# A two-layer block kernel: the mixer's attention moved ahead of its recurrence, and the first loads reordered

## The chip, the cores and the metric

The kernel runs on one core of one Trainium2 chip. The metric is the time of one execution on the device in microseconds (us); lower is better. Before the change the median of three runs is 2019.54 us (2014.81 to 2019.84).

## What is computed

One sequence of 256 tokens with 1024 features, in float32, goes through a first block of two layers and a second block of two layers. A layer of the first block is:

```
x = x + 0.5 * swiglu(rms_norm(x, g1), w_in, w_out)              # ffn1
z = rms_norm(x, g2) @ mix_w_in
z_fox, z_moba, z_rwkv = split(z)
y_fox  = forgetting attention: 4 heads of 64, q and k normed, causal softmax, cumulated log gates added
y_rwkv = recurrence: 8 heads of 64; per token  state = state*w + (state @ -kk) (kk*a)^T + v k^T,  y = state @ r
         then a norm per head, a bonus term and a gate
y_moba = attention: 4 heads of 64, q and k normed, rotary turn of 16 of 64 features, causal softmax
x = x + concat(y_fox, y_rwkv, y_moba) @ mix_w_out               # mixer
x = x + attention of x over 256 memory rows: 4 heads of 128     # xa
x = x + 0.5 * swiglu(rms_norm(x, g3), w_in, w_out)              # ffn2
```

The second block (convolution, sparse attention, pooling) is not touched.

## The kernel before, in words

**Weights.** All weights come as one stream of 546 units of 256 x 512 values (0.5 MB). SyncE loads unit u into one of four slots when VectorE is done with unit u - 4. Each product is made of three float32r matmuls (high by high, high by low, low by high), so a unit is split first: ScalarE copies the rounded high half (`act_split`, L296, which waits until TensorE has used unit u - 4), VectorE subtracts for the low half (`dve_split`, L305), and TensorE then runs twelve matmuls of 512 columns (L320 to L322) or twenty-four of 256 columns with the weights stationary (L343 to L345). The splits run three units ahead of TensorE when a stage begins.

**Order.** Each engine's program is written out by hand: `pe_mix`, `act_mix`, `dve_mix` and `pool_mix` list the steps of the mixer in the order in which the engine performs them, and semaphores tie them together. An engine stands still at a step until what the step waits for has come, whatever is ready behind it. So a `dve_split(1)` or `act_split(1)` in the list is a fixed place at which a unit is split, and what is behind it waits for TensorE to have used the unit four before.

**The mixer.** It takes 28 units for the projection, 8 for keys and values of the memory (`pe_kv`), 4 and 4 for the output (wo_a for the attentions, wo_b for the recurrence). The old order of the projection is: low-rank columns (4 units, `pe_rw_low`), the recurrence's k, r and v (12 units, `pe_rw_cols`, transposed output), then the attentions' q, k and v (12 units, `pe_z`). The recurrence is computed in four chunks of 64 tokens: key lengths (`pe_rw_length` L818, `dve_rw_length` L825, a power of -1/2 on GpSimd L830, `pe_rw_spread` L839), products of keys and queries (L924), the inverse of a triangular matrix per chunk by doubling (`pe_rw_inv0`, then `pe_rw_level` 1 to 5, L984, L993 and L996, with masks and additions on VectorE L1004 and L1009), then per chunk right-hand side, solution and state (`pe_rw_rhs`, `pe_rw_early`, `pe_rw_u`, `pe_rw_state`). In the old order the attention units lie between the levels, the memory's transposes (`pe_kv_turn`) and units and the first attention (fox) between the chunks, and the second attention (moba) behind the last chunk with nothing beside it, then wo_a and wo_b.

**Attention.** Norm of q and k (square, reduction L543, power on GpSimd L559, two scalings L551 and L554), rotary turn on 16 columns per head, transposes (L578) copied by ScalarE (L584), scores (L1333, for fox with added gate sums L1337), mask and maximum on VectorE (L1350, L591), exponentials on ScalarE (L599), transposes of the probabilities (L613) copied by ScalarE or VectorE (L620, L627), values (L641) and the final scaling (L649). Both attentions use the buffers of the recurrence's `BK` and PSUM banks 0 and 1.

**Three long steps on GpSimd.** "b end", "k end" (L889, L891) and the bonus product (L880), each over 1024 columns.

**The start.** ScalarE's queue loads the identity, half of x and the parameters, GpSimd's the constant tables (0.9 MB) and the positions; VectorE computes the rotary angles and ScalarE their sine (L1259) before ffn1.

## Time and profile before

| | us |
|---|---|
| median of 3 runs (lowest to highest) | 2019.54 (2014.81 to 2019.84) |
| the profiled execution, and its span | 2017.16, and 2015.9 |
| ffn1 of layer 0, to the end of its last unit | 210.5 |
| mixer of layer 0 / layer 1 | 284.4 / 280.8 |
| memory attention (xa) of layer 0 / layer 1 | 44.1 / 43.0 |
| second block, layer 0 / layer 1 | 285.6 / 289.4 |

The span runs from the first to the last instruction; the device's time adds 1.3 us. In a timeline row the first number is the start, the second the length; "xN" counts merged instructions, and the bracket gives the idle time before them and who ended it. Matmuls overlap, so the distance between two starts is the cost of one, not its length. The granted clock is a share of TensorE's full speed, 2.4 GHz; it has two levels, 1.0 and 0.5, and values between are means over a stretch.

### The profile page before, as it was taken

How to read it: one execution, taken by the hardware profiler on the slowest of the kernel's cores; microseconds unless marked ns; L12 is line 12 of the kernel's file. 1: busy time of each engine (PE TensorE's matmuls, PEld its weight loads, DVE VectorE, ACT ScalarE, POOL GpSimd, SP SyncE). 2: the span in 40 equal slices, each digit the busy share in tenths (PEclk: the TensorE clock that was granted, in tenths of full speed). 3: DMA queues.
4: the chain of work that ended last, by engine and by line, in shares of the span. 5: the costliest groups of instructions: out<-in, count | busy, mean ns of one | idle time of the engine just before them, and what ended most of it. 6: DMA issues, size and time to landing. Idle time of an engine off the chain costs nothing.

```text
span 2015.9 us, 28342 instructions
## 1 busy us (share of the span) xinstructions
PE 1912.3 (95%) x11756; PEld 1597.0 (79%) x11756; DVE 1184.9 (59%) x1673; ACT 927.4 (46%) x1409; POOL 112.3 (6%) x67
## 2 busy tenths in 40 slices
PE   6999899988899999998999889999999999999998
PEld 5888888767788878887887777788877888878887
DVE  4555476754555555554677445555577647586556
ACT  4444452334544454444523345444454654545553
POOL 0000020410000000000204100000010000010000
PEclk9999999898999999999999979999999999999999
DMA  5755341212355557553321123655445456444454
GB/s 198 245 188 188 117 124 65 74 43 84 119 174 188 188 165 246 188 188 124 119 85 63 54 84 113 200 189 189 162 136 165 143 189 208 147 148 164 148 189 134
DMA packets 83328, 299.19 MB, mean 148 GB/s; under 512 B 9600, under 2 KB 10752, under 8 KB 82944
## 3 DMA queue, kind: packets, MB, share of 16 engines
q1 hardware_dynamic: 79040, 287.87, 43.4%
q10 hardware_dynamic: 3840, 8.03, 1.1%
q8 instruction: 93, 1.52, 0.3%
q0 software_dynamic: 320, 1.48, 0.2%
q14 instruction: 35, 0.29, 0.0%
HBM read 296.30 MB, written 1.05 MB: 148 GB/s over the span
## 4 chain that ended last, share of the span: by engine, by line
PE 89%; DVE 7%; ACT 2%; issue 1%; DMA 1%; POOL 0%; SPq 0%; DVEq 0%; ACTq 0%
PE ps L320 23%; PE ps L322 22%; PE ps L321 22%; PE ps L343 2%; PE ps L345 2%; PE ps L344 2%; PE ps L641 1%; DVE wlo L305 1%; PE ps L450 1%; PE ps L993 1%; PE ps L578 1%; PE ps L368 1%; PE ps L984 1%; PE ps L996 1%; PE ps L1333 1%
## 5 line engine op out<-in xcount | busy, mean ns | idle before, releaser
L305 DVE TENSOR_TENSOR wlo<-raw,whi 128x1024 fp32r<-128x1024 f32 (+1 forms) x546 | 672.6, 1238 | 488.4 <-ACT whi L296 486.9
L296 ACT ACTIVATE whi<-raw 128x1024 fp32r<-128x1024 f32 (+1 forms) x546 | 573.1, 1054 | 475.4 <-PE ps L322 436.6
L320 PE MATMUL ps<-whi,a_hi 128*128 128x512 f32 x1632 | 658.2, 403 | 18.6 <-DVE wlo L305 16.9
L321 PE MATMUL ps<-wlo,a_hi 128*128 128x512 f32 x1632 | 643.5, 394 | 0.0
L322 PE MATMUL ps<-whi,a_lo 128*128 128x512 f32 x1632 | 643.4, 394 | 0.0
L320 PEld LDWEIGHTS ps<-whi,a_hi 128*128 128x128 f32 x1632 | 312.2, 191 | 91.0 <-issue 15.1
L322 PEld LDWEIGHTS ps<-whi,a_lo 128*128 128x128 f32 x1632 | 311.1, 191 | 67.9
L321 PEld LDWEIGHTS ps<-wlo,a_hi 128*128 128x128 f32 x1632 | 312.1, 191 | 61.4
L320 PE MATMUL ps<-whi,h_hi 128*128 128x512 f32 x384 | 149.9, 390 | 4.2 <-DVE h_lo L502 4.2
L322 PE MATMUL ps<-whi,h_lo 128*128 128x512 f32 x384 | 149.5, 389 | 0.0
L321 PE MATMUL ps<-wlo,h_hi 128*128 128x512 f32 x384 | 149.4, 389 | 0.0
L343 PE MATMUL ps<-a_hi,whi 128*128 128x256 f32 (+2 forms) x304 | 88.3, 290 | 0.0
L320 PEld LDWEIGHTS ps<-whi,h_hi 128*128 128x128 f32 x384 | 72.1, 188 | 19.9 <-DVE h_lo L502 5.1
L345 PE MATMUL ps<-a_hi,wlo 128*128 128x256 f32 (+2 forms) x304 | 85.8, 282 | 0.0
L344 PE MATMUL ps<-a_lo,whi 128*128 128x256 f32 (+2 forms) x304 | 85.7, 282 | 0.0
L322 PEld LDWEIGHTS ps<-whi,h_lo 128*128 128x128 f32 x384 | 72.1, 188 | 15.1
L321 PEld LDWEIGHTS ps<-wlo,h_hi 128*128 128x128 f32 x384 | 72.1, 188 | 14.8
L475 ACT ACTIVATE arena<-ps,small 128x256 f32<-128x256 f32 x88 | 36.9, 472 | 68.1 <-PE ps L322 68.1
L418 POOL TENSOR_TENSOR small<-small,minus_half 128x2 f32<-128x2 f32 x10 | 7.0, 701 | 1078.3 <-DVE small L411 701.6
L481 ACT ACTIVATE h_hi<-ps 128x256 fp32r<-128x256 f32 x88 | 29.1, 382 | 80.0 <-PE ps L450 80.0
L495 DVE SCALAR_TENSOR_TENSOR arena<-ps,small,arena 128x256 f32<-128x256 f32 x88 | 38.5, 479 | 44.7 <-ACT arena L475 44.7
L502 DVE TENSOR_TENSOR h_lo<-ps,h_hi 128x256 fp32r<-128x256 f32 x88 | 33.4, 420 | 46.5 <-ACT h_hi L481 46.5
(302 smaller groups left out, 1972.9 us busy)
## 6 DMA issues: line engine op xcount, KB each, us to landing
raw<-stream SPq DMA_DIRECT2D x546, 512.0 KB, 3.3
arena<-rows ACTq DMA_DIRECT2D x2, 1026.0 KB, 11.8
arena<-mem ACTq DMA_DIRECT2D x2, 1024.0 KB, 8.4
arena<-lora ACTq DMA_DIRECT2D x2, 768.0 KB, 6.0
arena<-rows ACTq DMA_DIRECT2D x2, 512.0 KB, 5.2
out<-x_res SPq DMA_DIRECT2D x1, 1024.0 KB, 4.0
const_tables<-consts POOLq DMA_DIRECT2D x1, 901.0 KB, 9.1
arena<-band POOLq DMA_DIRECT2D x1, 544.0 KB, 3.8
```

Of the source, the lines that this page charges most:

```text
L296: self.split_hi.mark(act.activation(self.weights(self.whi, u), self.weights(self.raw, u), ACT.Copy), u)
L305: self.split_lo.mark(dve.tensor_tensor(self.weights(self.wlo, u), self.weights(self.raw, u), self.weights(self.whi, u).bitcast(F32), ALU.s ...
L320: pe.matmul(out, a_h, hi, start=start, stop=False, skip_group_check=True)
L321: pe.matmul(out, a_h, lo, start=False, stop=False, skip_group_check=True)
L322: last = pe.matmul(out, a_l, hi, start=False, stop=True, skip_group_check=True)
L343: pe.matmul(out, hi, self.AHI[:, kt, :], start=first and kt == 0, stop=False, skip_group_check=True)
L344: pe.matmul(out, hi, self.ALO[:, kt, :], start=False, stop=False, skip_group_check=True)
L345: last = pe.matmul(out, lo, self.AHI[:, kt, :], start=False, stop=True, skip_group_check=True)
L475: self.silu.mark(act.activation(self.SG[:, t, :], self.bank(4 + t, 256), ACT.Silu, scale=self.rs(0, t)), key, j, t)
L481: self.ht_hi.mark(act.activation(self.HHI[:, kk, :], self.bank(6 + kk, S), ACT.Copy), key, j, kk)
L495: self.h_ready.mark(dve.scalar_tensor_tensor(self.H[:, t, :], self.bank(4 + t)[:, 256:512], self.rs(0, t), self.SG[:, t, :], ALU.mult, ALU ...
L502: self.ht_lo.mark(dve.tensor_tensor(self.HLO[:, kk, :], self.bank(6 + kk, S), self.HHI[:, kk, :].bitcast(F32), ALU.subtract), key, j, kk)
```

## The change

- **Projection order.** Behind the low-rank columns come the attentions' q, k and v (three groups of 4 units), then k, r and v of the recurrence; the host packs the weights so.
- **Attention beside the recurrence's units.** Both attentions run between the 12 units of the recurrence, on PSUM banks 2, 3 and 7, with buffers of their own in memory that the inverse uses later. The squares of q and k go from VectorE to ScalarE, and q and k are normed as two groups over both token halves. The second attention ends between the two halves of the key products.
- **The chain.** The memory's transposes stand between levels 1 to 3 of the inverse, its 8 units from level 4 on and between the chunks, transposes for wo_a in the last chunk and its units right behind; wo_b comes last.
- **Recurrence.** "b end", "k end" and the bonus product go from GpSimd to VectorE. The key products are reordered, with the same number of VectorE passes but for these.
- **Start.** On ScalarE's queue the parameters come before its half of x, and one split rather than three before the activations are turned. The tables' and positions' DMAs on GpSimd's queue are issued behind the first norm. Angles and sine go into the mixer of layer 0, the small parameter step into ffn1.

TensorE's and VectorE's orders, and what the prediction speaks of, from the diff (the removed lines of the orders are in the kernel before; ScalarE's order changes to match):

```diff
+        if l == 0 and f == "ffn1":
+            self.dve_split(AHEAD - 1)
         self.dve_rstd(key)
         for j in range(NJ):
+            if j == 2 and f == "ffn1":
+                self.dve_rw_params(l)
...
         pe = self.nc.tensor
-        pe.wait_ge(*self.rw_act("exp before", l, 1))
         pe.wait_ge(*self.rw_pool("length", l))
+        pe.wait_ge(*self.at_dve(("fox", l, 0), "out"))
...
+    def dve_rw_end(self, l, part):
...
+        if part == 0:
+            dve.wait_ge(*m("a w", l))
+            m.mark(dve.tensor_tensor(c4(self.E3), c4(self.BK[:, 0]), wc, ALU.mult), "b end", l)
+        else:
+            dve.wait_ge(*m("k w", l))
+            m.mark(dve.tensor_tensor(c4(self.E2), c4(self.BK[:, 1]), wc, ALU.mult), "k end", l)
...
+    def act_at_squares(self, l, q):
+        act, g = self.nc.scalar, 1 if q else 2
+        act.wait_ge(*self.z_act("z", l, g))
+        act.wait_ge(*self.z_dve("z", l, g))
+        if not q:
...
+        dve.wait_ge(*self.at_act("squares", l, q))
+        m.mark(dve.tensor_reduce(sm, self.asq.rearrange("p (h d) -> p h d", d=HD), AX, ALU.add), "sum", l, q)
+        dve.wait_ge(*m.last())
+        m.mark(dve.tensor_scalar(sm, sm, 1.0 / HD, EPS, ALU.mult, ALU.add), "mean", l, q)
...
+        if t == 0:
+            pe.wait_ge(*self.at_dve(*(("gained", l, False) if fox else ("roped", l, False))))
+            for sem, value in self.z_done(l, 3) if fox else [self.at_dve(("fox", l, 1), "out")]:
+                pe.wait_ge(sem, value)
+        for i, src in enumerate((ZQ, ZK)):
+            if t:
+                pe.wait_ge(*self.at_act(("turn", l, fox, i)))
...
+        queries, keys, values = (self.pe_z(l, g) for g in (1, 2, 3))
+        next(queries)
+        next(queries)
         self.pe_rw_lora(l)
+        next(queries)
+        next(queries)
         self.pe_rw_cum(l, 0)
         self.pe_rw_cum(l, 1)
+        for n in range(4):
+            next(keys)
+        for n in range(4):
+            next(values)
+        for sem, value in self.z_done(l, 2):
+            pe.wait_ge(sem, value)
         self.pe_rw_cols(l, 0, (0, 1))
+        self.pe_at_turn(l, True, 0)
+        self.pe_rw_cols(l, 1, (0, 1))
+        self.pe_at_turn(l, True, 1)
+        self.pe_rw_cols(l, 2, (0, 1))
+        self.pe_at_scores(l, True, 0)
+        self.pe_rw_cols(l, 3, (0, 1))
+        pe.wait_ge(*self.rw_act("exp before", l, 0))
+        self.pe_rw_cols(l, 0, (4, 5))
+        self.pe_at_probs(l, True, 0)
+        self.pe_at_values(l, True, 0)
+        self.pe_at_scores(l, True, 1)
+        self.pe_rw_cols(l, 1, (4, 5))
+        self.pe_rw_length(l)
+        self.pe_rw_cols(l, 2, (4, 5))
+        self.pe_rw_spread(l)
+        self.pe_at_probs(l, True, 1)
+        self.pe_at_values(l, True, 1)
+        self.pe_rw_cols(l, 3, (4, 5))
+        self.pe_at_turn(l, False, 0)
+        pe.wait_ge(*self.rw_dve("mixed", "k", l, 3))
+        self.pe_rw_cols(l, 0, (0, 1))
+        self.pe_at_turn(l, False, 1)
+        self.pe_at_scores(l, False, 0)
         self.pe_rw_cols(l, 1, (0, 1))
         self.pe_rw_cols(l, 2, (0, 1))
         self.pe_at_probs(l, False, 0)
         self.pe_at_values(l, False, 0)
         self.pe_at_scores(l, False, 1)
+        self.pe_rw_cols(l, 3, (0, 1))
+        self.pe_rw_products(l, 0)
+        self.pe_at_probs(l, False, 1)
+        self.pe_at_values(l, False, 1)
+        self.pe_rw_products(l, 1)
+        self.pe_rw_by_token(l, "v", self.VT, (0, 1), [self.rw_dve("mixed", "v", l, 3)])
+        self.pe_rw_inv0(l)
+        self.pe_kv_turn(l, 0, 2)
+        self.pe_rw_level(l, 1)
+        self.pe_kv_turn(l, 2, 2)
+        self.pe_rw_level(l, 2)
+        self.pe_kv_turn(l, 4, 2)
+        self.pe_rw_by_token(l, "b", self.E3, (0, 1), [self.rw_act("by token", "v", l, 1), self.rw_dve("b end", l)])
+        self.pe_rw_level(l, 3)
+        self.pe_kv_turn(l, 6, 2)
+        self.pe_rw_by_token(l, "k", self.E2, (0, 1), [self.rw_act("by token", "b", l, 1), self.rw_dve("k end", l)])
+        self.pe_kv(l, 0, 0)
+        self.pe_rw_level(l, 4)
+        self.pe_kv(l, 0, 1)
+        pe.wait_ge(*self.rw_act("by token", "k", l, 1))
+        self.pe_rw_bonus(l, 0)
+        self.pe_rw_gate(l, 0, 1)
+        self.pe_rw_level(l, 5)
+        pe.wait_ge(*self.rw_act("bonus", l))
+        self.pe_rw_gate(l, 1, 0)
+        self.pe_kv(l, 0, 2)
+        self.pe_rw_rhs(l, 0, 0)
+        self.pe_rw_early(l, 0, 0)
+        self.pe_rw_u(l, 0, 0)
+        self.pe_kv(l, 0, 3)
+        self.pe_rw_state(l, 0, 0)
+        self.pe_kv(l, 1, 0)
+        self.pe_rw_rhs(l, 0, 1)
...
+        self.pe_rw_rhs(l, 1, 1)
+        self.pe_rw_early(l, 1, 1)
+        self.pe_wo_a_turn(l, 0)
+        self.pe_rw_u(l, 1, 1)
+        self.pe_wo_a_turn(l, 2)
+        self.pe_rw_state(l, 1, 1)
+        for h in range(2):
+            self.pe_wo_a(l, h, 0)
+            self.pe_wo_a(l, h, 1)
         self.pe_turn(("wo_b", l), [[self.Y[:, t, k * P:(k + 1) * P] for t in range(NT)] for k in range(4)], (4, 5, 6, 7),
                      [self.rw_dve("out", l, 1)], kt0=4)
         for h in range(2):
             self.pe_gemm((2 * h, 2 * h + 1), 4, kt0=4, key=("wo_b", l), first=False)
...
         self.dve_rw_low(l)
+        self.dve_split(3)
         self.dve_at_tables(l, 0)
+        self.dve_split(1)
+        self.dve_z(l, 1)
+        self.dve_split(1)
+        self.dve_at_norm(l, True)
+        self.dve_split(1)
+        if l == 0:
+            self.dve_angles()
+        self.dve_at_scale(l, True)
         self.dve_split(2)
+        self.dve_at_rope(l, True)
+        self.dve_split(1)
+        self.dve_z(l, 2)
+        self.dve_split(1)
+        self.dve_at_norm(l, False)
+        self.dve_at_tables(l, 1)
+        self.dve_split(1)
+        self.dve_rw_rates(l)
+        self.dve_split(1)
+        self.dve_at_scale(l, False)
+        self.dve_split(1)
+        self.dve_z(l, 3)
+        self.dve_split(1)
+        self.dve_at_rope(l, False)
         self.dve_split(2)
         self.dve_at_scores(l, True, 0)
+        self.dve_split(1)
+        self.dve_rw_mix(l, "k", self.KT, (0, 1), PV_MUK)
+        self.dve_split(1)
         self.dve_at_probs(l, True, 0)
         self.dve_at_values(l, True, 0)
+        self.dve_split(1)
         self.dve_at_scores(l, True, 1)
+        self.dve_rw_length(l)
+        self.dve_rw_keys_k(l)
+        self.dve_split(1)
         self.dve_at_probs(l, True, 1)
+        self.dve_rw_keys(l)
         self.dve_at_values(l, True, 1)
+        self.dve_split(1)
+        self.dve_rw_mix(l, "r", self.RT, (4, 5), PV_MUR)
+        self.dve_split(1)
+        self.dve_rw_queries(l)
         self.dve_at_scores(l, False, 0)
+        self.dve_split(1)
+        self.dve_rw_keys_end(l)
+        self.dve_split(1)
         self.dve_at_probs(l, False, 0)
         self.dve_at_values(l, False, 0)
         self.dve_at_scores(l, False, 1)
+        self.dve_split(1)
+        self.dve_rw_mix(l, "v", self.VT, (0, 1), PV_MUV)
+        self.dve_rw_products(l, 0)
         self.dve_at_probs(l, False, 1)
         self.dve_at_values(l, False, 1)
+        self.dve_rw_products(l, 1)
+        self.dve_rw_inv0(l)
+        self.dve_kv_turn(l, 0, 2)
+        self.dve_rw_end(l, 0)
+        self.dve_rw_level(l, 1)
+        self.dve_kv_turn(l, 2, 2)
+        self.dve_rw_level(l, 2)
+        self.dve_kv_turn(l, 4, 2)
+        self.dve_rw_end(l, 1)
+        self.dve_rw_level(l, 3)
+        self.dve_kv_turn(l, 6, 2)
...
+        self.dve_rw_norm(l, 0)
+        self.dve_turn(("wo_a", l), 2, (2, 3))
+        self.dve_turn(("wo_a", l), 2, (2, 3), kt0=2)
+        self.dve_split(1)
+        self.dve_rw_centre(l, 1)
+        self.dve_split(1)
+        self.dve_rw_squares(l, 1)
+        self.dve_split(1)
+        self.dve_rw_norm(l, 1)
+        self.dve_split(1)
+        self.dve_turn(("wo_b", l), 4, (4, 5, 6, 7), kt0=4)
+        self.dve_split(1)
...
+        self.pool_at_norm(l, True)
+        self.pool_at_norm(l, False)
         self.pool_rw_length(l)
         self.pool_rw_clear(l)
         self.pool_rstd(("mem", l), 1)
         self.pool_rw_chunk(l, 0, 1)
+        self.pool_kv_norm(l)
+        self.pool_rw_chunk(l, 1, 0)
+        self.pool_rw_out(l, 0)
+        self.pool_rw_norm(l, 0)
         self.pool_rw_out(l, 1)
         self.pool_rw_norm(l, 1)
...
+        self.act_load1(0)
         act.dma_start(self.X[:, 1, :], a["x"].rearrange("(t p) d -> p t d", p=P)[:, 1, :]).then_inc(self.s_start, 16)
-        self.act_load1(0)
         act.wait_ge(*self.cleared("all"))
-        self.act_split(AHEAD)
-        self.act_angles()
+        self.act_split(1)
...
-        self.dve_split(AHEAD)
+        self.dve_split(1)
         for l in range(DEPTH):
-            self.dve_rw_params(l)
-            if l == 0:
-                self.dve_angles()
...
-        pool.dma_start(self.C[:, n:], a["consts"][:, n:]).then_inc(self.s_tables, 16)
-        pool.dma_start(self.POS, a["pos"]).then_inc(self.s_tables, 16)
         pool.wait_ge(*self.cleared("all"))
         for l in range(DEPTH):
             self.pool_rstd(("ffn1", l))
+            if l == 0:
+                pool.dma_start(self.C[:, n:], a["consts"][:, n:]).then_inc(self.s_tables, 16)
+                pool.dma_start(self.POS, a["pos"]).then_inc(self.s_tables, 16)
```

## Rows read from the trace of the kernel before

**Rows 1.** The page of the kernel before: span, and busy time by engine

```profile
span 2015.9 us, 28342 instructions
...
PE 1912.3 (95%) x11756; PEld 1597.0 (79%) x11756; DVE 1184.9 (59%) x1673; ACT 927.4 (46%) x1409; POOL 112.3 (6%) x67
```

**Rows 2.** Both mixers: stretch, length, busy us by engine (instructions), clock, DMA share, GB/s

```profile
211.80:496.20 284.40, 262.96 (x2580) 222.90 (x2580) 166.84 (x266) 110.58 (x202) 45.09 (x23) 0.90 0.26 82
924.40:1205.20 280.80, 258.99 (x2580) 220.26 (x2580) 166.67 (x267) 110.49 (x202) 45.10 (x23) 0.92 0.26 83
```

**Rows 3.** The same table, stretches of 10 us in layer 0's mixer

```profile
210.00:220.00 10.00, 5.56 (x26) 5.14 (x26) 4.03 (x10) 4.09 (x11) 0.70 (x1) 0.71 0.15 52
...
280.00:290.00 10.00, 6.00 (x26) 4.78 (x26) 10.00 (x5) 3.58 (x6) 8.28 (x3) 0.79 0.11 35
290.00:300.00 10.00, 10.00 (x96) 8.20 (x96) 7.89 (x12) 3.09 (x4) 0.00 (x0) 0.87 0.71 215
...
370.00:380.00 10.00, 7.59 (x65) 5.59 (x65) 4.46 (x12) 6.97 (x15) 4.38 (x2) 0.73 0.17 54
...
450.00:460.00 10.00, 7.17 (x29) 5.47 (x30) 4.68 (x11) 2.94 (x10) 0.00 (x0) 0.50 0.00 0
460.00:470.00 10.00, 6.76 (x29) 5.50 (x27) 4.50 (x11) 3.64 (x13) 0.00 (x0) 0.50 0.00 0
```

**Rows 4.** Timeline of the start: start, us, engine, line, operation, count, idle before

```profile
9.13 2.79 PE L368 MATMUL ps<-const_tables,x_res 128*128 128x128 f32 x12 [9.13 <-DMA x_res<-x]
9.18 1.06 ACT L296 ACTIVATE whi<-raw 128x1024 fp32r<-128x1024 f32 x1
10.34 1.22 DVE L305 TENSOR_TENSOR wlo<-raw,whi 128x1024 fp32r<-128x1024 f32 x1 [8.46 <-ACT whi L296]
...
17.36 0.23 ACT L1259 ACTIVATE small<-small 128x32 f32<-128x32 f32 x1 [2.71 <-DVE small L1253]
...
17.98 3.23 DVE L386 SCALAR_TENSOR_TENSOR a_lo<-ps,arena,a_hi 128x256 fp32r<-128x256 f32 x8 [0.66 <-ACT a_hi L375]
...
19.35 0.78 PE L320 MATMUL ps<-whi,a_hi 128*128 128x512 f32 x1
```

**Rows 5.** Timeline of ScalarE in layer 0's mixer

```profile
247.89 1.06 ACT L296 ACTIVATE whi<-raw 128x1024 fp32r<-128x1024 f32 x1 [0.55 <-PE ps L345]
248.97 1.28 ACT L792 ACT_TABLE_LOAD   x1
...
478.55 1.06 ACT L296 ACTIVATE whi<-raw 128x1024 fp32r<-128x1024 f32 x1 [1.66 <-PE ps L322]
481.27 1.06 ACT L296 ACTIVATE whi<-raw 128x1024 fp32r<-128x1024 f32 x1 [1.66 <-PE ps L322]
```

**Rows 6.** Timeline of VectorE in layer 0's mixer

```profile
276.93 1.23 DVE L853 TENSOR_TENSOR arena<-arena 128x1024 f32<-128x1024 f32 x1
...
302.22 0.69 DVE L1678 COPY arena<-ps 128x512 f32<-128x512 f32 x1 [0.84 <-PE ps L322]
...
312.10 2.49 DVE L975 TENSOR_TENSOR arena<-arena,const_tables 128x512 f32<-128x512 f32 x4
...
315.64 1.41 DVE L1004 TENSOR_TENSOR arena<-ps,const_tables 128x256 f32<-128x256 f32 x4
...
434.89 1.22 DVE L591 TENSOR_REDUCE small<-arena 128x4 f32<-128x1024 f32 x1
```

**Rows 7.** Timeline of GpSimd in layer 0's mixer

```profile
264.98 3.75 POOL L830 TENSOR_TENSOR small<-small,minus_half 128x16 f32<-128x16 f32 x1 [50.66 <-DVE small L825]
...
368.60 5.78 POOL L559 TENSOR_TENSOR small<-small,minus_half 128x16 f32<-128x16 f32 x2
```

**Rows 8.** Timeline of TensorE in layer 0's mixer

```profile
262.65 1.84 PE L818 MATMUL ps<-const_tables,arena 128*128 128x2 f32 x16
...
312.91 2.41 PE L984 MATMUL ps<-arena 64*64 64x64 f32 x64
...
446.03 1.83 PE L578 MATMUL ps<-const_tables,arena 128*128 128x128 f32 x8 [2.20 <-ACT arena L584]
```

More of the change, by code:

```diff
@@ new lines, in dve_rw_centre, with dve_rw_squares @@
+        dve.wait_ge(*self.rw_pe("y", l, t, 1))
+        m.mark(dve.tensor_reduce(MU, h3(self.bank(7)), AX, ALU.add), "gn sum", l, t)
+        dve.wait_ge(*m.last())
+        m.mark(dve.tensor_scalar(MU, MU, 1.0 / HD, None, ALU.mult), "gn mean", l, t)
+        dve.wait_ge(*m.last())
+        m.mark(dve.tensor_tensor(h3(self.Y[:, t, :]), h3(self.bank(7)), MU.unsqueeze(2).to_broadcast([P, 8, HD]),
+                                 ALU.subtract), "gn centred", l, t)
+    def dve_rw_squares(self, l, t):
+        dve, m, ss = self.nc.vector, self.rw_dve, self.var[t]
+        dve.wait_ge(*self.rw_act("gn square", l, t))
+        m.mark(dve.tensor_reduce(ss, self.GN.rearrange("p (h d) -> p h d", h=8), AX, ALU.add), "gn squares", l, t)
+        dve.wait_ge(*m.last())
+        m.mark(dve.tensor_scalar(ss, ss, 1.0 / HD, GN_EPS, ALU.mult, ALU.add), "gn var", l, t)
@@ new lines, in dve_at_rope @@
+    def dve_at_rope(self, l, q):
+        dve, m = self.nc.vector, self.at_dve
+        src = (ZQ if q else ZK) + 256
+        x = self.Z[:, :, src:src + 256].rearrange("p t (h d) -> p t h d", h=4)
+        x1, x2 = x[:, :, :, 0:8], x[:, :, :, 8:16]
+        cb, sb = (self.CS[:, :, i, :].unsqueeze(2).to_broadcast([P, NT, 4, 8]) for i in range(2))
+        v = self.atmp.rearrange("p (a t h d) -> p a t h d", a=3, t=NT, h=4)
+        dve.wait_ge(*self.at_act("sin"))
+        dve.wait_ge(*m("gained", l, q))
+        dve.tensor_tensor(v[:, 0], x2, sb, ALU.mult)
+        dve.tensor_tensor(v[:, 1], x1, sb, ALU.mult)
+        dve.tensor_tensor(v[:, 2], x2, cb, ALU.mult)
+        m.mark(dve.tensor_tensor(x1, x1, cb, ALU.mult), "products", l, q)
+        dve.wait_ge(*m.last())
+        dve.tensor_tensor(x1, x1, v[:, 0], ALU.subtract)
+        m.mark(dve.tensor_tensor(x2, v[:, 2], v[:, 1], ALU.add), "roped", l, q)
@@ L1385, in pe_kv_turn @@
+    def pe_kv_turn(self, l, k0, n):
         pe = self.nc.tensor
-        for what in (("bonus", l), ("gate", l, 0), ("gate", l, 1)):
-            pe.wait_ge(*self.rw_act(*what))
-        self.pe_turn(("mem", l), self.tiles(self.MEM), (2, 3), [(self.d_mem, 16 * (l + 1))])
-    def act_kv_turn(self, l):
-        self.act_turn(("mem", l), 8, (2, 3), self.PV[:, PV_MEM:PV_MEM + 8])
-        self.nc.scalar.wait_ge(*self.rw_act("square", l, 3))
+        if k0 == 0:
+            pe.wait_ge(self.d_mem, 16 * (l + 1))
+            pe.wait_ge(*self.at_dve(("moba", l, 1), "out"))
+        for k in range(k0, k0 + n):
+            if k >= 2:
+                pe.wait_ge(*self.turned_lo(("mem", l), k - 2))
+            for t in range(NT):
+                ins = pe.transpose(self.bank(2 + k % 2)[:, t * P:(t + 1) * P], self.MEM[:, t, k * P:(k + 1) * P],
+                                   self.c("ident"))
+            self.turned.mark(ins, ("mem", l), k)
@@ L1411, in act_kv @@
+        self.pe_unit([(self.bank(b + t), kk, 2 * n + kk, t, n == 0 and kk == 0) for kk in range(2) for t in range(NT)],
+                     self.AHI, self.ALO)
     def act_kv(self, l, part):
-        act, m = self.nc.scalar, self.kv_act
+        act, m, b = self.nc.scalar, self.kv_act, 0 if part else 2
         if part == 0:
@@ new lines, in pe_wo_a_turn @@
+    def pe_wo_a_turn(self, l, k0):
+        pe = self.nc.tensor
+        if k0 == 0:
+            pe.wait_ge(*self.kv_act(("kt", l, 1)))
+        for k in range(k0, k0 + 2):
+            if k >= 2:
+                pe.wait_ge(*self.turned_lo(("wo_a", l), k - 2))
+            for t in range(NT):
+                ins = pe.transpose(self.bank(2 + k % 2)[:, t * P:(t + 1) * P], self.Z[:, t, ZQ + k * P:ZQ + (k + 1) * P],
+                                   self.c("ident"))
+            self.turned.mark(ins, ("wo_a", l), k)
@@ new lines, in pe_mix @@
+        for n in range(4):
+            next(values)
+        for sem, value in self.z_done(l, 2):
+            pe.wait_ge(sem, value)
+        self.pe_rw_cols(l, 0, (0, 1))
+        self.pe_at_turn(l, True, 0)
[7 more added lines that the diff above has]
+        self.pe_at_probs(l, True, 0)
```

575 lines of the change are left out of this document (249 added, 326 removed).

## The prediction

> **What bounds the kernel now.** I read the page first. TensorE is busy for 95% of the span [rows 1]; the other engines matter only where TensorE waits for them, or idles so long that its clock falls. Next, the table of busy time by stage. The two mixers, the only stages that the change reorders, take 284.4 and 280.8 us, with TensorE idle for 21.4 and 21.8 us and a mean granted clock of 0.90 and 0.92 [rows 2]. The clock has two levels, 1.2 and 2.4 GHz; a mean of 0.90 is a fifth of the stretch at the lower one, some 57 us. The table in stretches of 10 us shows where [rows 3]: at the entry (210 to 220), after a wait of 4.0 us for VectorE and GpSimd (280 to 300), around the transposes of the memory (370), and from 446 to past 470, where the second attention runs with no weight unit beside it (0.50 in 450 to 470, TensorE busy for 7 us in 10). The entry's idle 4.4 us and its lower clock stay. What the change can touch in layer 0 is 21.4 - 4.4 = 17.0 us of idle time, and 57 less 5.8 at the entry, or 51 us, at the lower clock, of which about 12 are that idle time: the 39 of work would take half at full clock, 19 less. That makes 36 us in layer 0; by the same steps 17.4 + 16 = 33 in layer 1.
>
> **The start.** The first weight unit begins at 19.35 although x is there at 9.13, since ScalarE evaluates the sine of the rotary angles first, at 17.36, and only then copies the turned activations (VectorE follows at 17.98) [rows 4]. The change sends the angles into the mixer, and their tables behind the first norm. ScalarE then does one split, to 10.2; VectorE subtracts it, to 11.5; two low tiles of 0.40 us each (3.23 over 8) free two banks at 12.4, TensorE's last transposes take 0.6, and the first unit begins at about 13.0. Gain 6.3 us. Bounds: 5, if the shorter wait lets a later split bind; 8, if x lands earlier without 0.9 MB beside it. Those tables' DMAs are now issued at about 20 us and first read at 210; the weight stream beside them is four units deep, and I cost them at nothing. Without that cover they would cost up to their own transfer, 11 us at the mixer's mean of 82 GB/s [rows 2].
>
> **The mixer's work is the same.** TensorE has the same units and small matmuls in another order, so I count only waits and clock. Three VectorE operations of 1.14 us (start to start, [rows 6]) come from GpSimd, one square of 1024 columns goes to ScalarE. Prices: one unit is 2.72 us [rows 5]; a unit's slot is free for its successor-but-three only after TensorE has used it, and from there ScalarE's half takes 1.1 and VectorE's 1.2, 2.4 together. A VectorE pass over 1024 columns is 1.14, a dependent one or a reduction 1.25, a copy of 512 columns 0.65 [rows 6]. GpSimd's power over 16 columns is 2.9 to 3.75 us [rows 7].
>
> **The new waits**, in TensorE's order:
> - First query transposes. They need the values' copy on VectorE, behind this queue from the squares of the keys: four splits, reduction and mean, tables, two rate products, two scalings, the copy: 4.6 + 1.5 + 0.6 + 2.3 + 2.4 + 0.6 = 12 us. It starts after the key copy and ScalarE's square and split, 5.7 us behind the last key unit. TensorE has four value units and one recurrence unit, 14 us, to give: wait 3.7 us. In layer 0 the angles add about 1.2.
> - Spread of the key lengths. VectorE's scores stand behind the split whose slot the unit after the scores frees. Chain: 2.4 for the split, 2.8 for masks, maximum and shift (the reduction alone is 1.22 [rows 6]), 0.2, 3.75 for the power [rows 7], less the length matmuls of 1.84 [rows 8] and a unit of 3.0: wait 4.3; I take 3.9, as the power varies.
> - First blocks' probabilities wait behind ScalarE's split: 1.4 and, with the four "r k" copies also ahead, 2.6. Scores behind a split and a copy: 1.2. Last probabilities behind split, mix and exponentials on ScalarE and the masks on VectorE: 2.3. The output of the first attention: 0.3.
> - Inverse. Behind its eight products (2.7) and four additions of 0.6 come two turn subtractions, "b end" and the X masks before TensorE can go on [rows 6]. TensorE has the inversion, one transposing pair and four groups: wait 3.5. In the old order a unit lay there. Later levels follow without a wait.
> - End. "Centre" stands behind a split that needs the first wo_a unit used (5.1 us after the state), then 1.6, a split to 9.7, squares 0.9, the power of 8 columns some 2.5, a little less than the 2.9 of 16 [rows 7], three passes 2.1: wo_b's input is there at 15.2, its first low tiles two us later. Four wo_a units cover 11.1: wait 4.6 after taking off the transposes.
>
> - At nothing: GpSimd's output passes, now beside the chunks' VectorE work, since the last state needs neither for some 4 us; the DMAs inside the mixers are the same.
>
> Together 23.5 us in layer 1, 24.7 in layer 0. The lower clock after a wait: the 4.0 us before 287.8 left 0.79 and 0.87 in two stretches [rows 3], 6.8 us at the lower level, 1.9 of them idle, so 2.5 us lost; 2.2 us of idle time sufficed in another place [rows 8]. Waits of 1.4 us and less I cost at nothing. Five such events at 2.2 to 2.7 and one lost in the close series before it make 13 us, 1.6 more in layer 0. New cost per mixer: 36.5 and 39 against 33 and 36.
>
> **Sum.** 3.5 + 3 - 6.3 = +0.2 us, with 0.8 for eight memory units that now stand alone between small matmuls, +1. The profiled execution took 2017.2, the median is 2.4 above it; both give the median plus one: **2020.5 us**. The long half-clock stretch at 446 goes, and what is late in its place is spread over six waits.
>
> **A rule weighed.** A table load on ScalarE is 1.28 us and its neighbours follow without a gap: the split before it ends at 248.95, the load begins at 248.97 [rows 5]. The Trainium skill (ScalarE: Activation LUTs, What ACT_TABLE_LOAD costs) gives the same load but counts 1.38 us of drain with every switch of set. The trace does not agree here. By that rule the loads for exponential, logarithm and, in layer 0, sine, which the change puts ahead of the key copy, would each delay the first wait by up to 1.4 us more, and the sum would be +6 rather than +1.
>
> **Rivals.**
> - Faster, near 1990, chance 0.30: the clock hardly falls. In favour: there is a weight unit beside almost each attention step, as there is in the stretches that now run at 1.0. If the short waits shrink by half (to 16 us a mixer) and only the ends cost clock (5), a mixer costs 21, 12 to 15 less than now: -12 - 15 - 6 = -33, less a few for what the queues surely cost. Against: three of the waits are chains of fixed length counted from the last unit used.
> - Slower, near 2045, chance 0.17: the clock stays low through the inverse. Its place is the stretch from the inverse to the third level, where TensorE gets only transposes and 64-column matmuls (64 of them took 2.41 us [rows 8]) after a wait of 3.5 us. Twenty us of such work at the lower level costs 20, less 5 hidden in VectorE's queue: 12 to 15 more per layer, +25 to +30. It decides from the point where the clock does not come back by the second level. For it: at 450 to 470 it stayed at 0.50 over 20 us of small work and waits [rows 3]. Against: the old levels ran at full clock.
> - The start does not deliver, chance 0.08: x or the parameters land late, the first unit stays near 19: +6, or 2027.
> - My forecast's own case, chance 0.45, from 2010 to 2031.
>
> **From these the numbers.** The tables of this kernel tell 0.3%, 6 us, from no change. The forecast's case gives 0.07 faster, 0.28 same, 0.10 slower; the rivals add 0.30 faster, 0.17 slower, and the start 0.04 to either of the last two. Faster 0.37, same 0.32, slower 0.31. The range 1990 to 2037 leaves out half of the slow rival and some of the fast one.
>
> **What would show it.** First unit near 13 us; in each mixer TensorE waits of 3 to 5 us for VectorE at the first attention transposes, at the spread and at the level matmuls, and one of 4 before wo_b; GpSimd's three long operations gone and VectorE's 3.4 us pass back at 1.2; no stretch of 20 us at clock 0.50. A level stage at 0.5 shows the slow rival; a mixer under 272 us with clock over 0.95 the fast one. The prediction is wrong if the mixers change by more than 8 us each.

## The result, and the profile after

The changed kernel takes 2024.01 us (median of 20 runs, 2018.38 to 2027.36) against 2016.74 for the kernel before on the same chips: ratio 1.0033, 95% interval 1.0024 to 1.0042. It is slower by a third of a per cent, a small change whose interval is clear of 1; forecast were 2020.5 and a range of 1990 to 2037. One execution of the kernel before, at 5156 us, and one of the experiment `spread_later`, at 5299 us, stand far apart from all others, and the ratios leave them out. The median of before that the forecast started from, of three runs, was 2019.54; set against 2016.74 the change is 7.3 us, where 1 was said, and the profiled spans give 6.4. Its page, to be read beside [rows 1]; of its second part only the clock's line:

```profile
span 2022.3 us, 28312 instructions
...
PE 1911.6 (95%) x11756; PEld 1601.9 (79%) x11756; DVE 1170.3 (58%) x1645; ACT 929.7 (46%) x1413; POOL 91.3 (5%) x59
...
PEclk9999988999999999999988999999999999999999
```

TensorE is busy as long as before, 1911.6 us against 1912.3. GpSimd has lost 21 us and VectorE 15, and the time did not fall with them. The table by stage, both mixers with the columns of [rows 2] (the stretches run here from the last ffn1 matmul to the last wo_b matmul; each of [rows 2] is as long as one cut in this way):

```profile
205.00:492.40 287.40, 257.46 (x2574) 221.80 (x2575) 161.76 (x265) 112.04 (x202) 34.66 (x19) 0.93 0.25 82
918.30:1208.80 290.50, 262.54 (x2574) 225.84 (x2575) 159.50 (x251) 110.75 (x200) 34.64 (x19) 0.91 0.25 81
```

284.4 became 287.4, and 280.8 became 290.5. The start, TensorE alone, beside [rows 4]:

```profile
9.54 3.65 PE L379 MATMUL ps<-const_tables,x_res 128*128 128x128 f32 x16 [9.54 <-DMA x_res<-x]
12.83 0.78 PE L331 MATMUL ps<-whi,a_hi 128*128 128x512 f32 x1
```

The first unit runs 6.5 us earlier. For the rest I take each stage apart into three: TensorE's idle time, the time lost at the lower clock (half of what was spent at the lower level without being idle), and the remainder, called work. The half is a little too much, as the section on the prediction shows. They come from the intervals without a matmul and from the trace's record of the clock, whose means are the third figures from the end of the rows above.

| stage | length before, after | idle | lost at the lower clock | work |
|---|---|---|---|---|
| to the first unit | 19.4, 12.8 | | | |
| ffn1, layer 0 | 191.1, 192.2 | 3.9, 3.9 | 0, 1.7 | 187.2, 186.5 |
| mixer 0 | 284.4, 287.4 | 22.3, 30.0 | 22.0, 18.7 | 240.1, 238.7 |
| up to mixer 1 | 428.3, 425.9 | 12.6, 13.2 | 4.9, 1.7 | 410.8, 411.0 |
| mixer 1 | 280.6, 290.5 | 22.5, 28.0 | 17.8, 24.3 | 240.3, 238.2 |
| the rest | 806.7, 808.2 | 21.0, 20.8 | 11.6, 13.2 | 774.2, 774.2 |

The start gives 6.5, mixer 0 takes 3.0, mixer 1 takes 9.9, and the unchanged stages, together 0.1 to 0.2 us longer, changed by up to 2.4 each, mostly by clock. The long half-clock stretches of the kernel before, 27.3 us from 446.2 and 30.7 us from 1152.8, are gone, as forecast. Where the new idle time lies is in the timeline of TensorE in layer 0's mixer. In brackets stands the idle time before the row and who ended it. The rows have every wait of 0.8 us and more behind the entry but two, 0.98 before 356.49 and 0.88 before 359.94; some rows show only the first matmuls of their group:

```profile
276.48 1.09 PE L595 MATMUL ps<-const_tables,arena 128*128 128x128 f32 x4 [4.84 <-DVE arena L1767]
...
296.35 1.08 PE L658 MATMUL ps<-arena 128*128 128x64 f32 x8 [1.29 <-ACT arena L637]
...
322.47 1.76 PE L859 MATMUL ps<-const_tables,small 128*64 128x128 f32 x14 [4.50 <-POOL small L850]
...
337.74 0.72 PE L1405 MATMUL ps<-arena 64*128 64x128 f32 x8 [1.25 <-ACT arena L601]
...
347.71 1.08 PE L658 MATMUL ps<-arena 128*128 128x64 f32 x8 [2.84 <-ACT arena L637]
...
371.49 2.49 PE L1023 MATMUL ps<-arena 64*64 64x64 f32 x64 [1.66 <-DVE arena L1014]
375.55 0.34 PE L1032 MATMUL ps<-arena 64*64 64x64 f32 x4 [1.57 <-DVE arena L1043]
...
477.74 1.54 PE L379 MATMUL ps<-const_tables,arena 128*128 128x128 f32 x6 [4.27 <-DVE arena L1232]
```

They are the forecast's waits, nearly one by one. Where the clock is low, in stretches of 10 us as in [rows 3]:

```profile
270.00:280.00 10.00, 5.16 (x31) 4.99 (x30) 8.33 (x13) 2.18 (x4) 0.11 (x1) 0.74 0.59 183
290.00:300.00 10.00, 8.71 (x58) 7.32 (x57) 5.05 (x10) 7.11 (x19) 0.00 (x0) 0.93 0.38 125
300.00:310.00 10.00, 10.00 (x24) 6.11 (x23) 0.00 (x0) 0.00 (x0) 0.00 (x0) 0.50 0.00 2
310.00:320.00 10.00, 7.97 (x60) 7.76 (x58) 5.15 (x9) 2.57 (x8) 1.40 (x1) 0.89 0.17 52
320.00:330.00 10.00, 7.28 (x63) 6.77 (x64) 4.06 (x8) 2.10 (x5) 2.41 (x1) 0.83 0.17 54
350.00:360.00 10.00, 7.81 (x105) 7.00 (x104) 8.62 (x17) 4.95 (x14) 0.00 (x0) 1.00 0.14 52
```

The row to stop at is 300 to 310: TensorE is busy for all of it, with 18 of the first attention's 24 score matmuls and the first 6 of the next unit, and the clock stands at 0.50. By the clock's record the stretch goes from 298.6 to 312.2, 13.7 us; layer 1 has the same one from 1008.6 to 1022.2. The wait ahead of it is the 1.29 us one, which the forecast had costed at no clock.

### The profile page after: what moved, and what is told of

It reads as the page before. It is cut to its first block, busy times and chain, and to the rows that moved or that the text cites. A ratio compares the mean times of both kernels' runs of the same rounds, so it can differ in the third digit from the quotient of the medians.

```text
span 2022.3 us, 28312 instructions
## 1 busy us (share of the span) xinstructions
PE 1911.6 (95%) x11756; PEld 1601.9 (79%) x11756; DVE 1170.3 (58%) x1645; ACT 929.7 (46%) x1413; POOL 91.3 (5%) x59
## 3 DMA queue, kind: packets, MB, share of 16 engines
q0 software_dynamic: 320, 1.48, 0.2%
## 4 chain that ended last, share of the span: by engine, by line
PE 45%; DVE 5%; ACT 1%; issue 1%; POOL 0%; DVEq 0%; ACTq 0%
PE ps L331 11%; PE ps L333 11%; PE ps L332 11%; DVE wlo L316 1%; PE ps L658 1%; PE ps L595 1%; PE ps L2299 1%; PE ps L354 1%; PE ps L356 1%; PE ps L355 1%; PE ps L1032 1%; ACT whi L307 0%; PE ps L1409 0%; PE ps L1405 0%; PE ps L1035 0%
## 5 line engine op out<-in xcount | busy, mean ns | idle before, releaser
L354 PE MATMUL ps<-a_hi,whi 128*128 128x256 f32 (+2 forms) x304 | 92.8, 305 | 0.0
L386 ACT ACTIVATE a_hi<-ps,arena 128x256 fp32r<-128x256 f32 x96 | 39.8, 473 | 66.7 <-PE ps L1468 40.5
L354 PEld LDWEIGHTS ps<-a_hi,whi 128*128 128x128 f32 (+2 forms) x304 | 60.2, 198 | 1.5 <-issue 1.0
```

Source lines behind the costliest of these rows:

```text
L354: pe.matmul(out, hi, self.AHI[:, kt, :], start=first and kt == 0, stop=False, skip_group_check=True)
L386: self.turned_hi.mark(act.activation(self.AHI[:, kt0 + k, :], self.bank(banks[k % len(banks)], S), ACT.Copy, scale=gain[:, k:k + 1] if gai ...
```

## Experiments

The theory going in: the forecast's waits are right, and what is missing in the sum is clock. The rivals were that the order as such makes TensorE slow (narrow matmuls side by side), and that the operations moved from one engine to another do it. The last has no run of its own here. Every kernel ran in 4 to 12 timed executions beside the kernel before. The times are medians. A trace is of one execution, and where that one lies far from the median the text says so.

**The start alone**, in the old mixer order; the angles go beside the inverse there. VectorE's lines; ScalarE's queue is changed to match, and the tables' DMAs move as in the change:

```
-        self.dve_split(AHEAD)
...
-                self.dve_angles()
+        self.dve_split(1)
...
         self.dve_at_tables(l, 1)
+        if l == 0:
+            self.dve_angles()
```

> The mixer stays in its old order; only the start is the new one (angles evaluated beside the inverse of layer 0's mixer, their tables loaded behind the first norm). Theory (the start gives its 6.3 us and the new mixer takes more than that back): first weight unit at about 13 instead of 19.35, layer 0's mixer as before within 1.5 us, time about 6 us under the kernel before, 2011. Rival (the later loads and the sine inside the mixer cost as much as the start wins): same as before within 2 us, the difference visible as a longer first feed-forward or first mixer.

2014.27 us, ratio 0.9993 (0.9981 to 1.0005): the first unit at 12.21, 7.1 us earlier, but the total only 2.4 lower, which the interval does not tell from nothing. Mixer 0 is 2.1 longer, with a new wait of 1.5 us before the inverse, behind the angles on VectorE. Mixer 1, in which nothing was changed, is 3.7 us longer: its idle time is the same 22.5, its loss at the lower clock 21.7 instead of 17.8. The theory's 6 us did not come. The rival was nearer, with a longer first mixer, but the larger loss came in layer 1, which it did not name: the start's gain is real where it is made, and part of it was gone elsewhere.

**The mixer alone**, with the old start.

> The new mixer with the old start. Theory (the mixers alone cost what the profile of the changed kernel shows: 3.0 us in layer 0, 9.9 in layer 1): first unit near 19.3, waits the same as in the changed kernel within 0.5 us each except the first query transposes of layer 0 (3.5 instead of 4.8 since no angles are in the queue), and about 12 us over the kernel before, 2029; the half-clock time of a mixer changes by several us with nothing in the mixer changed but the moment at which it starts. Rival (layer 1's extra 6.5 us of clock loss come from the order itself, not from where the waits fall): layer 1 again 10 us longer, layer 0 again 3, each within 1.5.

2027.61, ratio 1.0048 (1.0026 to 1.0070). Every wait is there, the first query transposes at 3.44 in both layers. Mixer 1 is 290.5 again, as the rival had it; mixer 0 is 289.4, with 23.9 us lost at the lower clock instead of 18.7, and 27.4 idle. The order costs 5 and 10 us here; the 3 of layer 0 in the changed kernel were a lucky case. (The traced execution took 2031.9; the twelve lie between 2012.5 and 2036.0.)

**One line on ScalarE**, the first block's copy ahead of the split:

```
-        self.act_split(1)
         self.act_at_probs(l, True, 0)
+        self.act_split(1)
         self.act_rw_keys(l)
```

> One line: ScalarE copies the first block's probabilities before it splits the next unit instead of after. Theory (the 1.29 us wait before the first block's values, which the forecast costed at no clock, is what the 13.7 us half-clock stretch behind it hangs on): wait 1.29 to 0.4, and if the stretch goes with it, 6 us per mixer, 2012; Rival (the stretch comes from the narrow score matmuls behind it): only the 0.9 us of wait per mixer goes, 2022, and the half-clock stretch stays at 13.7.

2010.96, ratio 0.9976 (0.9962 to 0.9990), 13 us under the changed kernel for half a microsecond of idle time per mixer. Its timeline, with the length matmuls of the changed kernel (313.15) and of this one (305.84), and its stretches, the second pair in layer 1:

```profile
295.30 1.08 PE L658 MATMUL ps<-arena 128*128 128x64 f32 x8 [0.78 <-ACT arena L637]
```

```profile
313.15 1.85 PE L838 MATMUL ps<-const_tables,arena 128*128 128x2 f32 x16
```

```profile
305.84 1.84 PE L838 MATMUL ps<-const_tables,arena 128*128 128x2 f32 x16
```

```profile
290.00:300.00 10.00, 9.22 (x60) 7.49 (x59) 4.65 (x9) 7.17 (x19) 0.00 (x0) 1.00 0.32 108
300.00:310.00 10.00, 10.00 (x72) 8.86 (x71) 2.84 (x6) 1.06 (x1) 0.00 (x0) 1.00 0.06 21
1000.00:1010.00 10.00, 9.22 (x47) 6.41 (x47) 4.53 (x8) 4.68 (x11) 0.00 (x0) 1.00 0.31 105
1010.00:1020.00 10.00, 8.01 (x67) 7.75 (x65) 5.15 (x9) 2.53 (x7) 1.35 (x1) 1.00 0.16 55
```

The stretch at 0.50 is gone in both layers. What it cost can be read without any split of terms. From the start of these values to the start of the length matmuls TensorE has the same work and no wait: 16.80 us in the changed kernel (296.35 to 313.15), 10.54 here, so 6.3 us less; in layer 1 the same. (The 10 us from 300 hold 72 matmuls where they held 24, but not of the same kinds.) The two mixers together got 10.7 us shorter, 4.1 and 6.6: in layer 0 other low stretches, from 342.2 and from 366.1, took part of it back.

**Work of no use in that wait**, order unchanged:

```
         self.pe_at_probs(l, True, 0)
+        pe.wait_ge(*self.rw_act("exp before", l, 1))
+        self.pe_fill(6, 4)      # 4 matmuls of 512 columns, dead bank
         self.pe_at_values(l, True, 0)
```

> The changed kernel in its own order, with four matmuls of 512 columns into a dead bank in the 1.29 us wait before the first block's values, and nothing else. Theory (those 1.3 us of standing still are what the 13.7 us half-clock stretch needs): the copy arrives when it did, so no idle time is won, but the stretch goes in both layers and the time falls as with the earlier copy, to 2012. Rival (the earlier copy helped by what it moved on ScalarE, or the narrow score matmuls bring the clock down by themselves): the stretch stays, 2022 to 2025.

2009.91, ratio 0.9971 (0.9957 to 0.9984), 14 us under the changed kernel:

```profile
293.87 0.60 PE L635 MATMUL ps<-const_tables,arena 128*128 128x128 f32 x4
294.23 1.18 PE L595 MATMUL ps<-a_hi 128*128 128x512 f32 x4
295.76 1.08 PE L663 MATMUL ps<-arena 128*128 128x64 f32 x8 [0.35 <-ACT arena L642]
```

```profile
300.00:310.00 10.00, 10.00 (x70) 8.70 (x70) 2.42 (x5) 1.06 (x1) 0.00 (x0) 1.00 0.03 4
```

The values start 1.89 us after the transposes ahead of them (293.87), as in the changed kernel, so nothing was won by an earlier copy. Of 1.29 us of standing still 0.35 was left, and the 13.7 us at half clock were gone. That rules out both the narrow matmuls by themselves (they are the same 24 behind it) and ScalarE's order. The Trainium skill (TensorE: Matmul & The Clock Gate, A second HAM failure mode: psum-queue depth-cycling) tells of a kernel whose frequent short stops between groups of matmuls swung the clock. This trace shows the clock low behind a single such stop, of 1.29 us.

**Filling five waits**: the first query transposes, spread, the second attention's values, first level, wo_b's transposes.

One of the five:

```
+        self.pe_fill(0, 16)
         self.pe_rw_spread(l)
```

> The changed kernel; before five waits of each mixer (first query transposes, spread, values of the second attention's first block, first level, wo_b's transposes) TensorE multiplies 13, 16, 10, 6 and 15 times over 512 columns into a dead bank, about 0.23 us each at full clock, so less than each wait. Theory (the clock falls because TensorE stands still, and what it costs is the 17 to 23 us of each mixer that its half-clock stretches take): the waits' length stays, half-clock stretches at these five places go, 24 us or more off, 2000 or less. Rival (it is the attention's narrow matmuls that bring the clock down, whatever stands before them): the stretch at 0.50 of 13.7 us behind the first block's values stays, and the gain is under 8 us.

2004.41, ratio 0.9927 (0.9903 to 0.9951). The gain is 20 us where 24 were expected. The traced execution took 1995.28, 9 us under the median, so its mixers are the good case:

```profile
202.20:476.10 273.90, 257.02 (x2635) 221.50 (x2635) 161.12 (x265) 111.63 (x203) 34.66 (x19) 0.99 0.26 86
...
901.80:1180.70 278.90, 263.52 (x2634) 225.71 (x2635) 159.19 (x251) 110.33 (x200) 34.65 (x19) 0.96 0.26 84
990.00:1000.00 10.00, 10.00 (x25) 5.33 (x24) 0.83 (x3) 0.87 (x3) 0.00 (x0) 0.58 0.19 65
```

Here the wait of 1.29 us before the values was left alone. In layer 0 no low stretch followed it, in layer 1 the 13.7 us one did (the row from 990). So that wait is enough for it, but does not bring it every time. Over all traces: four kernels have the wait of 1.28 or 1.29 us (the changed one, the mixer alone, and this one twice), and the 13.7 us stretch stands behind it in 6 of their 8 mixers. With the wait at 0.78 (seven kernels) or 0.35 (the filled one) it stands in none of 16. A mere shift in time, which every edit also makes, would not sort them so. The kernel was run once more, beside others:

> The same kernel as the one with five fills in the changed order, run again beside the others on one chip: if the fills hold the clock, 2004 within 3 us again.

1999.92, ratio 0.9914 (0.9895 to 0.9933), 4.5 us off the first series where 3 were said; the intervals of the ratios overlap. Single executions of this one kernel go from 1994.5 to 2007.3.

**Taking waits away by order.** Each on top of the earlier copy (2010.96). First the end of the mixer, on VectorE and in the same way on ScalarE:

```
         self.dve_turn(("wo_a", l), 2, (2, 3), kt0=2)
-        self.dve_split(1)
         self.dve_rw_centre(l, 1)
-        self.dve_split(1)
         self.dve_rw_squares(l, 1)
-        self.dve_split(1)
+        self.dve_split(2)
         self.dve_rw_norm(l, 1)
```

> On top of the earlier copy of the first block's probabilities: at the mixer's end VectorE centres the last state and ScalarE squares it before they split the next units, not after. Theory (the 4.27 us wait before wo_b is a chain that hangs on the split which needs the first wo_a unit used): wait 0 to 1 in both layers, the half-clock stretch of 6.8 us behind it shorter or gone, 8 to 11 us under the kernel with the earlier copy alone, about 2001. Rival (GpSimd's power and its output passes are late too and take the chain's place): wait still over 2.5 us, gain under 4.

1997.13, ratio 0.9908 (0.9893 to 0.9924), 13.8 us less, where 8 to 11 were expected. VectorE in the changed kernel, then in this one (the traced execution took 1991.49, 6 us under the median):

```profile
466.44 1.23 DVE L316 TENSOR_TENSOR wlo<-raw,whi 128x1024 fp32r<-128x1024 f32 x1 [4.07 <-ACT whi L307]
467.58 0.68 DVE L1209 TENSOR_REDUCE small<-ps 128x8 f32<-128x512 f32 x1
```

```profile
451.76 0.76 DVE L395 TENSOR_TENSOR a_lo<-ps,a_hi 128x256 fp32r<-128x256 f32 x2 [1.15 <-ACT a_hi L386]
452.55 0.69 DVE L1209 TENSOR_REDUCE small<-ps 128x8 f32<-128x512 f32 x1
```

It stood still for 4.07 us behind a split with the state's sum ready to be taken. Without that, wo_b's transposes wait for nothing; 0.61 us is left before its first unit. The 6.8 us low stretch there is gone as well.

Second, the rate products behind the values' copy:

```
-        self.dve_rw_rates(l)
         self.dve_split(1)
         self.dve_at_scale(l, False)
         self.dve_split(1)
         self.dve_z(l, 3)
+        self.dve_rw_rates(l)
```

> On top of the earlier copy: VectorE's two rate products stand behind the values' copy instead of ahead of it. Theory (the first query transposes wait for that copy alone, at the end of VectorE's queue): wait 4.8 to 2.5 in layer 0 and 3.4 to 1.1 in layer 1, 4.6 us off in idle time and up to 5 more in clock, about 2004. Rival (the keys' scaling, which waits for GpSimd's power, is as late as the copy): less than 1 us off each wait.

2008.15, ratio 0.9963 (0.9949 to 0.9976), 2.8 less. The waits went to 2.87 and 1.48 (1.96 off each, of 2.3 expected); the clock gave nothing, though 5 were hoped for: its loss went from 16.4 to 18.8 us in layer 0 and from 18.7 to 17.1 in layer 1.

Third, the spread later, with the keys' passes on VectorE behind the block's output:

```
-        self.pe_rw_spread(l)
         self.pe_at_probs(l, True, 1)
         self.pe_at_values(l, True, 1)
         self.pe_rw_cols(l, 3, (4, 5))
+        self.pe_rw_spread(l)
```

> On top of the earlier copy: TensorE spreads the key lengths after the second block's values and the last r unit, no longer ahead of them, and VectorE takes the keys' passes behind that block's output. Theory (power of 16 columns and the queue before it end 4.5 us too late only for the old place): wait before the spread 4.5 to 0, its half-clock stretch gone; the probabilities in its place wait up to 1.5; the keys' passes, 4 us later, delay nothing for more than 1 us: 5 to 10 us under the earlier copy alone, about 2003. Rival (the wait moves: the passes now end too late for the second attention's transposes, values or the products): a new wait of 2 us or more behind it and a gain under 3.

2011.52, ratio 0.9969 (0.9951 to 0.9987): no gain in the median. The executions fall into two groups, four from 2001.9 to 2004.8 and six from 2009.4 to 2013.2, and the traced one, 2001.92, is the lowest, so its rows show this order at its best. The wait of 4.5 became three:

```profile
309.88 0.66 PE L630 MATMUL ps<-const_tables,arena 128*128 128x128 f32 x4 [1.67 <-ACT arena L616]
310.87 0.66 PE L630 MATMUL ps<-const_tables,arena 128*128 128x128 f32 x4 [0.33 <-ACT arena L616]
312.29 3.59 PE L658 MATMUL ps<-arena 128*128 128x64 f32 x16 [0.77 <-ACT arena L637]
```

The probabilities wait for ScalarE's exponentials, which had been hidden behind the spread's wait. Idle time falls by 1.3 and 2.4 us, and a low stretch of 6.8 us stands at this spot in both layers. The rival has the size right (a gain under 3, waits of over 2 us in place of the old one), but not the cause: the second attention's transposes now wait for nothing, and its first values wait 2.60 us, less than before (2.84).

**All moves together**, with two more: the bonus copies on ScalarE later, and "b end" behind level 1.

> The three moves and two more: the four bonus copies on ScalarE go behind the memory's turn (wait before the values of the second attention's first block 2.84 to 1.2), and VectorE's 'b end' behind level 1 (the two waits there, 3.2 together, to 2). If waits are simply additive, 4.3 + 2.3 + 4 + 1.6 + 1.2 = 13 us of idle time per mixer goes, and half of each half-clock stretch that hangs on them, some 10 per mixer: about 1968. Rival (short waits that stay keep the clock low all the same, or the moved work lands on the next step): 1985 or more.

1980.55, ratio 0.9829 (0.9808 to 0.9850). Its mixers, in an execution of 1975.22 us, 5 under the median:

```profile
202.00:471.70 269.70, 251.09 (x2575) 218.09 (x2575) 161.63 (x266) 112.03 (x203) 33.78 (x19) 0.96 0.26 87
897.60:1161.90 264.30, 246.69 (x2575) 214.02 (x2575) 159.50 (x251) 110.66 (x201) 33.76 (x19) 0.97 0.27 89
```

Idle time is 18.6 and 17.6 us, 11.3 and 10.4 less than in the changed kernel (13 expected), and the clock loses 11.5 and 6.6. The time is between the two texts. The clock still loses where waits stay: 4.5 at the entry, 2.9 and 1.5 before the first transposes, and 0.8 to 1.7 elsewhere.

> The five moves without that of the spread, which by itself turned one wait of 4.5 us into three of 2.8 together. Theory (the spread's move is worth only that 1.7 us and its clock): 2 to 8 us over the kernel with all moves, 1983 to 1989. Rival (with the other moves made, the spread's own wait of 4.5 is the last big one and brings a longer half-clock stretch with it): more than 8 over, 1990 or later.

1981.32, ratio 0.9818 (0.9805 to 0.9830): leaving the spread where it was changes nothing that these series can tell. Theory and rival both had it slower than all moves, by 2 us or more; that did not show.

**Moves and filling**, four places; 34 extra matmuls per mixer.

> All moves, and TensorE multiplies into a dead bank while it waits: 16 times over 512 columns at the mixer's entry (wait 4.46), 6 times each before the first query transposes, the second block's probabilities and the first level. Theory (standing still brings the clock down, so work of no use in a wait holds it): the stretch of 3.4 us at the entry goes and that at 308.9 shrinks, idle time falls with the fill, the mixers are 3 to 6 us shorter each, about 1971. Rival (the waits that are left, 0.8 to 1.7 us, are enough by themselves): under 3 us in all.

1971.96, ratio 0.9765 (0.9753 to 0.9778), the fastest here: 44.8 us under the median of the kernel before in the first series, and 8.6 under the moves alone. (Against its own series' kernel before it is 47.2.) Its mixers:

```profile
205.20:468.50 263.30, 251.76 (x2609) 216.79 (x2609) 161.42 (x266) 111.61 (x202) 33.76 (x19) 0.99 0.27 89
895.60:1159.60 264.00, 254.39 (x2609) 219.45 (x2608) 159.25 (x252) 110.33 (x200) 33.75 (x19) 0.97 0.26 89
```

They take 263.3 and 264.0 us, 6.4 and 0.4 less than in the trace without the fill. Idle time fell by 7.1 and 8.0 us, but the work of no use put 8.7 and 7.7 in its place, about as much. The gain is clock, and it came in layer 0 alone: 3.4 us lost instead of 11.5, in layer 1 6.5 instead of 6.6. So 3 to 6 us for each mixer did not come as expected; the total of 1971 did. How much of the 8.6 us is chance is open: the two traced spans are only 3.3 apart, and that without the fill is of an execution 5 us under its median.

## Why the prediction was right, and where it was not

- **The start.** 13.0 forecast, 12.83 measured. The gain in place was 6.5 (6.3 forecast); 1.1 of it went in ffn1, where a short stretch at the lower clock stood that the old start did not have.
- **The waits.** Forecast, then layer 0 and layer 1: first transposes 3.7 (and 1.2 for the angles), 4.84 and 3.43; first values 1.4, 1.29 and 1.28; spread 3.9, 4.50 twice; output of the first attention 0.3, 0.3 and 0.6; scores of the second 1.2, 1.25 twice; its first values 2.6, 2.84 and 2.85; last probabilities and values 2.3, 2.2 and 1.6; levels 3.5, 3.23 twice; end 4.6, 4.27 twice. Idle time without the entry's 4.5 and 4.4, which the kernel before has too: 25.5 and 23.5 where 24.7 and 23.5 were said. The spread was short by 0.6; 0.4 of it I had taken off my own chain of 4.3 for a power that varies, and it took 3.81. 0.4 us before the first memory unit I had not seen.
- **The clock**, the term that was mis-sized. I wrote 13 us a mixer, 1.6 more in layer 0; without the entry's 1.7 it was 17.0 and 22.6. The step that failed is "waits of 1.4 us and less I cost at nothing": the one of 1.29 brought 13.7 us at half clock in both layers, with TensorE busy throughout, so 6.8 us each by half, and 6.3 by the clocked distance in the experiment with the earlier copy. The forecast's 13.8 on average and these 6.8 make 20.6; measured were 19.8 on average. That they meet so well is luck: the other stretches cost 10.2 us in layer 0 and 15.8 in layer 1, where 14.6 and 13 were said. Both runs that touch only that wait fit the size: 13 and 14 us less for two mixers, and in the first the clocked distances make 12.6 for the stretches and 1.0 for the waits.
- **What made it up.** TensorE's work was 1.3 and 2.1 us less than before, where I had put 0.8 on top for the memory units that stand alone. Part of that is the way of counting. Behind the 1.29 us wait the units' matmuls of 256 columns start every 0.213 us at the lower level and every 0.120 at the higher, a factor of 1.78 and not 2, so half of the time at the lower level is more than was lost. The traces bear it out: with 6.6 us lost (all moves, layer 1) the work is 240.2, with 24.3 lost 238.2. Whether all of the fall is that is open. In layer 0 all terms together give 3.0 as forecast, and with the mixer alone 5.0, so the match is luck. In layer 1 they give 9.9 for 3.5, past the 8 us that the text set as its mark of an error for each mixer. The total still lay in the forecast's own case, since the other layer was cheap and the first experiment shows how much of such a sum is chance.
- **Table loads.** The row speaks as before: three passes of ScalarE without a gap around two loads, at 253.66 and 255.18.

```profile
253.46 0.19 ACT L1367 ACTIVATE small<-small 128x8 f32<-128x8 f32 x1
253.66 1.28 ACT L1369 ACT_TABLE_LOAD   x1
254.96 0.21 ACT L1369 ACTIVATE small<-small 128x8 f32<-128x8 f32 x1
255.18 1.28 ACT L1342 ACT_TABLE_LOAD   x1
256.48 0.23 ACT L1342 ACTIVATE small<-small 128x32 f32<-128x32 f32 x1
```

  The 1.38 us of drain that the Trainium skill (ScalarE: Activation LUTs, What ACT_TABLE_LOAD costs) adds to each switch does not show: two switches take 2.8 us from 253.66 to 256.48. (The prediction's price for it is short: five loads of up to 1.4 us would make +8, not +6. Nothing hangs on it.)
- **The rivals.** The fast one (the clock hardly falls) is refuted for this order; a clock that hardly falls is what all moves with filling come near, in layer 0. The slow one was right that clock is lost on small work after a wait, and wrong about the place: the levels ran at 1.0 in layer 0 from 366.9 on, in layer 1 they had 3.4 us at 0.50 (from 1090.5), and the long low stretch came 70 us earlier, in the scores.

## What to carry to other kernels

Forecast waits from the queue that ends them, and do not price the clock by a wait's length: one of 1.3 us, ahead of narrow matmuls that take 6.5 us at full clock and a unit, cost 6.3 us in clock in six places of eight, while behind the one of 4.5 us ahead of the spread at most half of a 6.8 us stretch was lost. That what runs behind a wait decides it is a guess; no run here put other work behind the same wait. Before reordering for overlap, look in each queue for a stage's split or copy that stands ahead of the one operation that TensorE waits for; two such moves were worth 27 us here. And where a wait can't be taken away, a few matmuls into a dead bank can keep the clock: four for each mixer were worth 14 us, though thirty-four on top of the better order gained nothing in layer 1.

## What was not expected of the hardware

- The same program loses more or less at the lower clock from one execution to the next. Of 20 executions of the changed kernel the span went from 2017.1 to 2026.1 us and the mean granted clock from 0.971 to 0.964, the longer ones with the lower clock (correlation -0.82; about 1 us for each thousandth). The kernel before goes from 2010.3 to 2022.4 without its one outlier, so the three runs from which the forecast started could tell its median only within some us. With the mixer alone the times went from 2012.5 to 2036.0. A single profile therefore can't carry a difference of 5 us (those of two experiments here lie 9 us under their medians), and a change of moment ahead of an unchanged stage moves that stage: mixer 1 by 3.7 us in the first experiment.
- Behind idle time of 1.3 us 13.7 us at 1.2 GHz followed in six mixers of eight. Behind 0.8 us at the same place no low stretch stood within the next 10.5 us, up to the length matmuls, in any of the fourteen mixers of the seven profiled kernels that have the earlier copy.
